# RMS-norm statistics in a hybrid backbone layer: pairs of squares added by Pool before the ones-matmul

## The reference

```python
def rmsnorm(x, g):
    xf = x.astype(jnp.float32)
    y = xf * lax.rsqrt(jnp.mean(xf * xf, axis=-1, keepdims=True) + EPS)
    return (y * g.astype(jnp.float32)).astype(x.dtype)

def block(x, mods, ...):
    h = rmsnorm(x, norm_ffn1) * (1.0 + m(1)) + m(0)
    x = x + 0.5 * m(2) * swiglu(h, w1_ffn1, w3_ffn1, w2_ffn1)
    h = rmsnorm(x, norm_mix) * (1.0 + m(4)) + m(3)
    mix, s_f, s_b = mixer(h, ...)        # gated linear attention both ways, short gated convolution
    x = x + m(5) * mix
    h = rmsnorm(x, norm_ffn2) * (1.0 + m(7)) + m(6)
    x = x + 0.5 * m(8) * swiglu(h, w1_ffn2, w3_ffn2, w2_ffn2)
    return x, s_f, s_b
# afterwards: y = rmsnorm(x, final_norm)
```

## Time and profile before

| | us |
|---|---|
| median of 3 runs | 1367.88 |
| lowest, highest | 1333.22, 1456.43 |
| profiled execution, device time | 1334.19 |
| profiled execution, span of the slowest core (core 6) | 1332.7 |
| spans of the 8 cores | 1324.1 to 1332.7 |
| mean granted TensorE clock, by core | 0.985 to 0.990 |
| busy: PE, DVE, ACT, Pool | 1260.2, 519.2, 380.0, 179.9 |

### The profile page before, as it was taken

The page is one execution under the profiler, slowest core; times in us unless marked ns, Lnnn a source line. Parts: engine busy times, 40 slices in busy tenths (PEclk is TensorE's granted clock), DMA queues, the critical chain, the costliest instruction groups (busy, mean ns, idle before and its releaser), DMA issues.

```text
span 1332.7 us, 18779 instructions; the slowest of 8 cores (1324.1 to 1332.7 us)
## 1 busy us (share of the span) xinstructions
PE 1260.2 (95%) x6592; PEld 570.7 (43%) x6592; DVE 519.2 (39%) x794; ACT 380.0 (29%) x625; POOL 179.9 (13%) x300
## 2 busy tenths in 40 slices
PE   2699999999998999899999989999999999999996
PEld 1244444444444444344444334444444444444442
DVE  2143243211331345576366645531243212432446
ACT  3354100111001244766435325621100111001343
POOL 3122001000010000123324222310001000000000
PEclk9899999999998999999999989999999999999998
DMA  9985456422569310002412213622313111020223
GB/s 176 224 185 79 80 85 94 76 32 32 91 92 151 97 64 1 1 1 53 76 24 51 86 37 90 110 49 42 59 27 62 34 32 32 0 48 1 61 63 130
DMA packets 33835, 90.93 MB, mean 68 GB/s; under 512 B 3888, under 2 KB 8400, under 8 KB 31568
## 3 DMA queue, kind: packets, MB, share of 16 engines
q0 software_dynamic: 21792, 62.01, 28.8%
q1 hardware_dynamic: 11952, 27.73, 6.4%
HBM read 137.04 MB, written 14.68 MB: 114 GB/s over the span
## 4 chain that ended last, share of the span: by engine, by line
PE 87%; DMA 5%; DVE 3%; issue 2%; ACT 2%; POOL 1%; DVEq 0%; ACTq 0%; SPq 0%; POOLq 0%
PE ps L235 87%; DMA sb_arena<-w_ada 3%; DVE sb_arena L263 2%; ACT sb_arena L248 2%; DMA sb_arena<-x 1%; DVE sb_arena L252 1%; PE ps L239 0%; POOL sb_arena L232 0%; POOL sb_arena L257 0%; ACT L248 0%; DVE sb_arena L730 0%; POOL sb_arena L252 0%; DVEq L141 0%; DVEq L1136 0%; ACTq L141 0%
## 5 line engine op out<-in xcount | busy, mean ns | idle before, releaser
L235 PE MATMUL ps<-sb_arena 128*128 128x512 bf16 (+4 forms) x5792 | 1204.1, 368 | 13.1 <-DVE sb_arena L252 5.4
L235 PEld LDWEIGHTS ps<-sb_arena 128*128 128x128 bf16 (+3 forms) x5792 | 534.9, 98 | 671.1 <-issue 62.2
L248 ACT ACTIVATE sb_arena<-ps 128x512 f32<-128x512 f32 (+3 forms) x272 | 161.1, 600 | 749.5 <-PE ps L235 743.6
L252 DVE TENSOR_TENSOR sb_arena<-sb_arena,ps 128x512 bf16<-128x512 f32 (+1 forms) x208 | 143.0, 688 | 505.3 <-PE ps L235 403.0
L263 DVE SCALAR_TENSOR_TENSOR sb_arena<-ps,sb_der,sb_arena 128x512 f32<-128x512 f32 x192 | 144.1, 751 | 160.7 <-PE ps L235 160.7
L248 ACT ACTIVATE sb_arena<-sb_arena 128x512 bf16<-128x512 f32 (+2 forms) x184 | 115.2, 678 | 39.3 <-DMA sb_arena<-x 17.7
L232 POOL DMA_DIRECT2D sb_arena<-w_ffn x88 | 47.1, 545 | 440.2 <-PE ps L235 410.1
L252 DVE TENSOR_TENSOR sb_arena<-sb_arena 128x512 f32<-128x512 f32 x96 | 64.5, 713 | 22.4 <-ACT sb_arena L248 22.4
L259 POOL TENSOR_SCALAR sb_arena<-sb_arena,sb_der,sb_modT 128x512 bf16<-128x512 f32 x44 | 39.8, 907 | 223.8 <-DVE sb_arena L252 192.7
L235 PE MATMUL ps<-sb_arena,sb_onesB 128*128 128x512 bf16 x144 | 42.4, 406 | 27.2 <-ACT sb_arena L248 25.5
L248 ACT ACTIVATE sb_arena<-sb_arena,sb_modT,sb_der 128x512 bf16<-128x512 f32 x48 | 39.0, 812 | 69.1 <-DVE sb_arena L252 55.5
(11 more groups left out here) (40 smaller groups left out, 157.7 us busy)
## 6 DMA issues: line engine op xcount, KB each, us to landing
sb_arena<-w_ffn POOLq DMA_DIRECT2D x44, 512.0 KB, 7.6
sb_arena<-w_ada POOLq DMA_DIRECT2D x36, 512.0 KB, 9.3
sb_arena<-w_ffn POOLq DMA_DIRECT2D x44, 256.0 KB, 9.9
sb_arena<-x SPq DMA_DIRECT2D x8, 1024.0 KB, 13.4
y<-sb_arena SPq DMA_DIRECT2D x32, 256.0 KB, 3.6
xspill<-sb_arena SPq DMA_DIRECT2D x4, 1024.0 KB, 3.9
sb_arena<-xspill SPq DMA_DIRECT2D x4, 1024.0 KB, 5.9
sb_arena<-w_cv POOLq DMA_DIRECT2D x12, 256.0 KB, 7.9
```

The lines of the kernel that those rows point to most:

```text
L235: return P.add("pe", lambda e: e.matmul(out, lhsT, rhs, start=start, stop=stop), reads=flat(reads), writes=flat(writes))
L248: return P.add("act", lambda e: e.activation(out=out, in_=in_, func=func, **kw), reads=flat(reads), writes=flat(writes))
L252: return P.add(eng, lambda e: e.tensor_tensor(out=out, in0=in0, in1=in1, op=op), reads=flat(reads), writes=flat(writes))
```

## The change

The eight bf16 buffers of squares become four. A slice of two squares now writes fp32 into two of the four buffers at `TMP`, and a Pool `tensor_tensor` adds the two into one bf16 buffer at `SQ`. The statistics are four matmuls over the four sums. The list keeps its 14 slices: the first of the two statistics slices is empty, and all four matmuls stand in the second, with Ln and Exp behind them. All 16 norms use this; the heads' norm in the mixer (16 further ones-matmuls, `onorm_b`) is not touched.

```diff
             def squares(k0, n):
-                if k0 == 0:
-                    st["sq"] = [P.alloc("sq%d" % kc, SQ + kc * KB, KB) for kc in range(8)]
-                for kc in range(k0, k0 + n):
-                    act(bf(SQ + kc * KB, 512), xv(kc, blk), AF.Square, [t_x[kc][blk]], [st["sq"][kc]])
+                i = k0 // 2
+                if i == 0:
+                    st["sq"] = [P.alloc("sq%d" % j, SQ + j * KB, KB) for j in range(4)]
+                two = []
+                for kc in (k0, k0 + 1):
+                    o = TMP + (kc % 4) * 2 * KB
+                    t = P.alloc("tmp%d" % (kc % 4), o, 2 * KB)
+                    act(f32(o, 512), xv(kc, blk), AF.Square, [t_x[kc][blk]], [t])
+                    two.append((f32(o, 512), t))
+                (a, t_a), (b, t_b) = two
+                tt("pool", bf(SQ + i * KB, 512), a, b, ALU.add, [t_a, t_b], [st["sq"][i]])
 
             def stats(k0, n):
                 for kc in range(k0, k0 + n):
-                    mm(ps[:, 7, :], onesB[:], bf(SQ + kc * KB, 512), kc == 0, kc == 7, [t_ones, st["sq"][kc]], [t_ps[7]])
-                if k0 + n == 8:
+                    mm(ps[:, 7, :], onesB[:], bf(SQ + kc * KB, 512), kc == 0, kc == 3, [t_ones, st["sq"][kc]], [t_ps[7]])
+                if k0 + n == 4:
...
-            out += [lambda: stats(0, 4), lambda: stats(4, 4)]
+            out += [lambda: None, lambda: stats(0, 4)]
```

## The result

| | us |
|---|---|
| changed kernel, median of 4 runs | 1350.45 (1349.40 to 1512.51) |
| kernel before, median of 4 runs | 1352.05 (1333.22 to 1456.43) |
| ratio, changed to before | 1.0118, 95% interval 1.0098 to 1.0138 |
| profiled execution, before and after | 1334.19, 1349.40 |
| spans of the 8 cores, before and after | 1324.1 to 1332.7, 1340.0 to 1347.9 |

The change makes the kernel 1.2% slower, about 16 us. The forecast was 1343, 9.3 us over the profiled execution's time.

A forecast was written before the change was run, and what follows sets the result against it. PE was taken to bound the kernel (busy 95% of the span). Losses of +16.05 and gains of −11.0 made +5, the clock +4.3: +9.3 on the profiled 1334.19 gave 1343 us, range 1331 to 1377.

The forecast's parts named there:

- Seven covered norms: Mixer, second-FFN and final norms whose adds end before PE needs them: 0.86 us gained each, −6.0 together.
- the exposed ones: Norms in both FFNs where PE must wait for Pool's adds: losses of +0.8 to +4.65 us each.
- the tail: Last norm, with nothing behind it: +3.3 us, +2.0 without Pool and DVE contending for SBUF.
- the mixer's last norm: Norm inside first pass over heads' inputs: v unit's matmuls run in the bank 7 wait, −5.0 us; 2.6 at full clock.
- Norms 3 and 4 of the first FFN: Squares come right ahead of the statistics, so PE waits for the last add: +0.8 us each.
- The second norm and the start: First FFN's start: first norm 0; second norm +1.4 us, since x arrives late and PE already waits.
- The second FFN's norms 2 to 4: Short units and Pool's weight DMA issues ahead of the adds: +2.1, +3.0 and +4.65 us, before any clock loss.
- The clock's part: PE dropping to 1.2 GHz after three new waits in the second FFN: +4.3 us, from 0 to 10.
- the ten issues: Second FFN, norm 4: eight w2 and one pair of weight DMA issues on Pool delay its adds; loss +4.65 us.
- All adds are hidden: Rival, chance 0.10: 12 norms gain 0.86 us and the first heads' pass 5.0, −15.4 in all, 1319 us.
- The moved slot gives nothing: Rival, chance 0.12: PE waits in the next heads' unit instead, so −5.0 becomes −0.86; 1347 us.
- Slower, by the clock: Rival, chance 0.14: five new FFN waits each bring a stretch at 1.2 GHz, 3.4 us each; +22, 1356 us.

The follow-up runs named there:

- the run without the scalings: Changed kernel with DVE's last six scalings of the block before the last left out; time not comparable, tail costs 3.1 us and not 3.6.
- slot-only kernel: Kernel before, with its eight bf16 squares and eight statistics matmuls, only the first statistics slot emptied and all eight put in the second; ratio 0.9989.
- the kernel with bf16 squares: Changed kernel with squares written as bf16 into eight buffers of their own, Pool adding two bf16 tiles; ratio 1.0078 to the kernel before.

## Why the prediction was right and wrong

*Direction and sign by norm: right.* Seven covered norms gain (−6.4 us measured, −6.0 told), the mixer's last gains by its slot, and the exposed ones and the tail lose. Each of the three places that I named as large is large.

*The sum: 5 us short*, +14.2 by core and +15.2 for the slowest core, against +9.3. Two steps failed: the gain of the mixer's last norm was read from one core (point 1), and the chain from square to last matmul was reckoned without its handoffs (points 2 and 4). Point 3 is a size, and 1.5 us were put at nothing (between the stages, and behind the last Ln).

1. *The mixer's last norm*, −5.0 told, −3.6 measured as a mean. I read the gain from the profiled core, and that core had dropped to 1.2 GHz there. It did gain 5.4 us. But a wait of 3.6 us stood on all eight cores, and the drop followed it on four (cores 3, 5, 6 and 7, which gain 3.4 to 5.4); core 0, at full clock in both traces, gains 2.5. The slowest core lies 4.4 us above the mean of the eight before and 4.7 after, and it is another one each time: core 6 then, core 5 afterwards, whose start and mixer ran longer. So what a stage is worth to the time is its mean over the cores. The number 2.6 for a core at full clock stood in the prediction, and the term had to lie between the two.
2. *Norms 3 and 4 of the first FFN*, +0.8 told, +1.2 measured each (1.29 and 1.16). I had taken 1.2 us from the first square to the first add and nothing from an add to the square that waits for it. The rows show 1.41 (79.39 to 80.80), an idle Pool of 0.33 and 0.24 ahead of adds 2 and 3, and 7.18 us for the chain that I had at 6.7.
3. *The second norm and the start*, +1.4 told, +2.4 measured; on core 6 it was 1.8. The cores differ by 0.4 to 4.1, by when x lands, and kernels that leave these norms as they were differ by up to 1.4 in the mean, so I can't say more of the remainder. The first norm by itself cost nothing, as told: its last matmul starts 1.7 us after the last square and not 0.1, and PE's work behind it waited for weights in both.
4. *The tail*, +3.3 told, +3.6 measured, and this is close by luck: 2.0 was for the chain and 1.3 for contention, and the run without the scalings shows 2.6 to 3.1 and 0.5 to 1.0. The handoffs of point 2 are in it, for there too the chain is squares, two turns of buffers, and adds.

*The second FFN's norms 2 to 4: right in sum, not in parts.* 14.05 with the clock, 14.2 measured. The clock's part was 3.7 (4.3 told), the chains' 10.5 (9.75 told). But of norm 4 I had said that the ten issues make it; with them gone it lost 4.6 of 6.2. So this step had the wrong cause: the chain from the first square, which starts late on ACT, carries most of it.

*Between the stages*, told 0, +1.1 us: mostly the mixer, whose stretches at 1.2 GHz fall otherwise in every execution, on some cores for the better. Behind the last Ln, where the outputs leave, it is +0.4 as a mean.

*The median.* The sum was made against the profiled execution's 1334.19, so the ratio of 1.0118 is to be held against its +0.7%, and 1343 not against the median 1367.88 that was shown: beside that median 1343 reads as a gain, and the kernel is slower.

*The rivals.* "All adds are hidden" falls with 49.4 us of waits for Pool. "The moved slot gives nothing" falls with the slot-only kernel. "Slower, by the clock" is half true: a drop follows the waits of the second FFN's norms 3 and 4 on all eight cores and of norm 2 on two, and none follows norms 3 and 4 of the first FFN.

*Left open:* how the eight buffers and the faster add share what the kernel with bf16 squares gains (3.3 us in norms 2 and 3 of the second FFN); why the start lost 1 us more than reckoned.

## What to carry to other kernels

Halving the work of the bounding engine by adding a step on another engine pays only where the new chain (here square, square, add, four in a row, with the buffers' turns) ends before the engine comes for it; of 16 norms 8 had that, and putting the change into those alone turned +1.2% into −0.6%. Two more with moved slots came to −0.8%, which the intervals do not tell from −0.6%. Reckon such a chain with every handoff (0.14 to 0.34 us each here), from the first operation and not from the last. Where the added step can go on a faster engine with a free queue, that alone took the whole loss away here (adds on DVE, 0.69 us for 1.27). And a gain that is read from one core is that core's: look at the same stage on the others, and take the mean.

## What the runs showed of the hardware that was not expected

- Waits of PE of 0.74 to 1.23 us, four in a row with one matmul between (norm 3 of the second FFN), were followed by 3.4 us at 1.2 GHz on every core; no single long wait stood there. With matmuls of no use in the gaps the clock stayed at 2.4 GHz.
- The same wait of 3.6 us ahead of the mixer's last norm, on all eight cores of the kernel before, was followed by time at 1.2 GHz on four of them (granted clock 0.72 to 0.86 from 562 to 574) and by none on the other four (1.00).
- DVE with two SBUF operands and Pool with two, at once: Pool's add 1.71 us and not 1.26, DVE's scaling up to 1.75 and not 0.75. DVE's additions and multiplications with one operand in PSUM beside Pool's adds kept their 0.69.
- Pool adds two bf16 tiles in 1.14 us at least, two fp32 ones in 1.25.
- Between 70 and 90 us some runs show a granted clock of 0.81, neither of the two levels above, for 6 to 14 us on end, while PE was busy without a wait. The slot-only kernel on core 0, and the kernel before on its core 0:

```profile
75.00:87.00 12.00, 12.00 (x48) 4.95 (x46) 1.70 (x3) 7.66 (x13) 0.00 (x0) 0.81 1.05 223
```

```profile
75.00:87.00 12.00, 12.00 (x58) 5.46 (x56) 1.58 (x3) 9.24 (x15) 0.00 (x0) 1.00 1.06 212
```

It stands in all four kernels that ran on one chip (on every core, over the 20 us 0.86 on cores 0 to 3, 0.92 to 0.96 on the others), on six cores of the two that ran on a second, and in none of the four on a third nor in the two first traces. So it goes with the chip and the core, and not with the kernel. It cost up to 2 us; what calls it forth no run here shows.
